# Input norm moved into the state-space input projection, and four staging places in the tail of a hybrid decoder block

## The reference

```python
u = rms_norm(h, norm_g[l])
proj = u @ w_in[l]
q, f_logit, iv, g_hg, u_s, z_s, gate_hg, gate_s5 = jnp.split(proj, _split_points(), axis=-1)
o = hgrn2_mix(...)                      # 8 heads of 128, chunks of 64 steps
y_hg = (rms_norm(o, hg_norm_g) * silu(g_hg)) @ w_o_hg[l]
ys = gelu(s5_mix(u_s, ...))             # 32 groups of 16 channels, 64 complex states each
ys = glu_a * sigmoid(glu_b) * silu(z_s) # glu_a, glu_b from ys @ w_glu + b_glu
y_s5 = ys @ w_o_s5[l]
h = h + (sigmoid(gate_hg) * y_hg + sigmoid(gate_s5) * y_s5) @ w_out[l]
h = h + (p[l] @ w_ple[l]) * sigmoid(rms_norm(h, ple_norm_g[l]) @ w_ple_gate[l])
return rms_norm(h, final_norm_g)
```

## Time and profile before

| | us |
|---|---|
| median of 3 runs | 2375.37 (2375.15 to 2377.81) |
| the profiled execution | 2378.16 |
| its span in the trace | 2376.6 |
| PE busy | 2272.8 (96%) |
| DVE busy | 1199.0 (50%) |
| ACT busy | 919.9 (39%) |

### The profile page before, as it was taken

The page is one execution under the profiler, slowest core; times in us unless marked ns, Lnnn a source line. Parts: engine busy times, 40 slices in busy tenths (PEclk is TensorE's granted clock), DMA queues, the critical chain, the costliest instruction groups (busy, mean ns, idle before and its releaser), DMA issues. The chain is left out here.

```text
span 2376.6 us, 30201 instructions
## 1 busy us (share of the span) xinstructions
PE 2272.8 (96%) x10800; PEld 1836.9 (77%) x10800; DVE 1199.0 (50%) x2230; ACT 919.9 (39%) x1360; POOL 146.8 (6%) x254
## 2 busy tenths in 40 slices
PE   6899999999999997999999999969999999999997
PEld 2688888888888886888777777758887777778775
DVE  5443444343444434111656566546566566665655
ACT  6343444443444434111233333333443354354343
POOL 0000000000000000110111111110001000100100
PEclk8899999999999999999999999989999999999998
DMA  4110101010100100322222222265336435634622
GB/s 160 36 36 23 45 9 44 9 49 18 35 26 26 41 18 14 86 65 85 78 78 87 87 77 80 77 202 167 118 114 212 153 99 177 212 107 135 219 90 79
DMA packets 89267, 206.37 MB, mean 87 GB/s; under 512 B 20832, under 2 KB 30048, under 8 KB 89184
## 3 DMA queue, kind: packets, MB, share of 16 engines
q1 hardware_dynamic: 68432, 139.68, 18.7%
q0 software_dynamic: 20752, 65.57, 8.3%
HBM read 157.87 MB, written 46.14 MB: 86 GB/s over the span
## 5 line engine op out<-in xcount | busy, mean ns | idle before, releaser
L95 PE MATMUL s_ps<-u_hi,s_w_hi 128*128 128x512 f32 x768 | 305.4, 398 | 8.7 <-DVE s_w_lo L875 8.7
L96 PE MATMUL s_ps<-u_lo,s_w_hi 128*128 128x512 f32 x768 | 300.0, 391 | 0.0
L97 PE MATMUL s_ps<-u_hi,s_w_lo 128*128 128x512 f32 x768 | 299.5, 390 | 0.0
L95 PE MATMUL t_ps<-t_oa_hi,t_w_hi 128*128 128x512 f32 x512 | 205.1, 401 | 13.8 <-DVE t_oa_lo L1555 9.9
L96 PE MATMUL t_ps<-t_oa_lo,t_w_hi 128*128 128x512 f32 x512 | 203.0, 396 | 2.5 <-issue 2.5
L97 PE MATMUL t_ps<-t_oa_hi,t_w_lo 128*128 128x512 f32 x512 | 202.7, 396 | 0.0
L1446 DVE TENSOR_TENSOR t_w_lo<-c_raw,t_w_hi 128x1024 fp32r<-128x1024 f32 x136 | 166.5, 1224 | 63.4 <-ACT t_w_hi L1352 63.4
L95 PEld LDWEIGHTS s_ps<-u_hi,s_w_hi 128*128 128x128 f32 x768 | 144.4, 188 | 52.6 <-issue 14.5
L97 PEld LDWEIGHTS s_ps<-u_hi,s_w_lo 128*128 128x128 f32 x768 | 144.5, 188 | 31.1
L96 PEld LDWEIGHTS s_ps<-u_lo,s_w_hi 128*128 128x128 f32 x768 | 144.6, 188 | 28.5
L1352 ACT ACTIVATE t_w_hi<-c_raw 128x1024 fp32r<-128x1024 f32 x136 | 142.4, 1047 | 41.7 <-PE t_ps L97 13.2
(11 more groups left out here) (280 smaller groups left out, 4786.6 us busy)
## 6 DMA issues: line engine op xcount, KB each, us to landing
c_raw<-w_in_in SPq DMA_DIRECT2D x56, 512.0 KB, 3.7
gates_scratch<-s_stage POOLq DMA_DIRECT2D x64, 256.0 KB, 2.7
t_ein<-gates_scratch SPq DMA_DIRECT2D x64, 256.0 KB, 4.4
c_raw<-w_o_hg_in SPq DMA_DIRECT2D x32, 512.0 KB, 5.0
c_raw<-w_out_in SPq DMA_DIRECT2D x32, 512.0 KB, 3.5
c_raw<-w_ple_gate_in SPq DMA_DIRECT2D x32, 512.0 KB, 3.5
c_raw<-w_glu_in SPq DMA_DIRECT2D x16, 512.0 KB, 4.2
t_xa<-o_gated_scratch POOLq DMA_DIRECT2D x32, 256.0 KB, 4.3
```

The source lines that it names most:

```text
L95: pe.matmul(out, w_hi, u_hi, start=first, stop=False)
L96: pe.matmul(out, w_hi, u_lo, start=False, stop=False)
L97: return pe.matmul(out, w_lo, u_hi, start=False, stop=last)
```

## The change

Two parts.

**The head.** `phase_norm_in` is gone; `phase_head` does the norm and the four `u_s` blocks inside the first block of the hgrn phase. x for all 2048 steps lies in `x_xs` (64 KB a partition), is normalised in place, and `u_lo` has the same place in SBUF. For time tile t, TensorE first projects blocks 0 and 1 (into `hg_pf`, `hg_pg`), taking slice k of both as soon as `u_lo` of that slice is there, then blocks 2 and 3 (into `hg_pi`, `hg_pq`). ScalarE drains the four into `n_stage`, and SP stores them. The squares of tile 0 are still summed over all slices by TensorE; those of tiles 1 to 3 are added up by VectorE first (L638, seven additions a tile), so that one matmul with the ones is left a tile, put between slices 2 and 3 of blocks 2 and 3. All four blocks' weights are held at once (two in `c_raw`, two in `n_raw_b`), and the loads of head 0's weights go out in between. The table for Ln and Exp is loaded before the first square. `phase_s5` starts with the `z_s` blocks and has 20 slots.

**The tail.** `t_xa` has four places instead of two, and the waits of its loads follow the split that frees the place.

```diff
-def phase_norm_in(nc, c, a, u_hi, u_lo):
+def phase_head(nc, c, a, xs, u_hi, u_lo):
...
+            for i in range(FIRST):
+                ks = slice(i * KT // FIRST, (i + 1) * KT // FIRST)
+                sp.dma_start(xs[:, ks, 0:TT], a["x"][:, ks, 0:TT]).then_inc(first_in[i], 16)
+            for i in range(2):
+                sp.dma_start(raw[:, i], a["w_in"][UB + i]).then_inc(raw_in[i], 16)
...
+            def normed_blocks(t):
+
+                for half in range(2):
+                    pair = (2 * half, 2 * half + 1)
+                    if t == 0:
+                        pe.wait_ge((w_lo_done, w_lo_b_done)[half], 2)
+                    else:
+                        pe.wait_ge(u_staged, (t - 1) * S5KT + pair[1] + 1)
+                    for k in range(KT):
+                        if half == 0:
+                            pe.wait_ge(lo_done, t * KT + k + 1)
+                        elif k == 3 and t + 1 < NT:
+                            pe.wait_ge(added, (t + 1) * (KT - 1))
+                            pe.matmul((pk, pv)[(t + 1) % 2][:], c["ones"][:].bitcast(F32), sumsq[:, (t + 1) % 2],
+                                      start=True, stop=True).then_inc(xms_done, 1)
+                        for b in pair:
+                            ins = split_matmuls(pe, (pf, pg, pi, pq)[b][:], w_hi[:, b, k], w_lo[:, b, k],
+                                                u_hi[:, k, tile_of(t)], u_lo[:, k, tile_of(t)], k == 0, k == KT - 1)
...
+            for t in range(1, NT):
+                for k in range(KT):
+                    round_u(t, k)
+                    if t + 1 < NT:
+                        square(t + 1, k)
+                    if k == 2:
+                        drain(t - 1, 2)
+                        drain(t - 1, 3)
+                for kind in range(2):
+                    drain(t, kind)
+                    if t == NT - 1:
+                        round_weights(0, kind)
+                if t + 1 < NT:
+                    one_over_rms(t + 1)
...
+            def add_square(t, k):
+                dve.wait_ge(sq_done, t * KT + k + 1)
...
+                before = sq[:, 0] if k == 1 else sumsq[:, t % 2]
+                dve.tensor_tensor(sumsq[:, t % 2], before, sq[:, k % 4], ALU.add).then_inc(added, 1)
...
+            for t in range(NT):
+                dve.wait_ge(xrstd_done, t + 1)
+                for k in range(KT):
+                    normalise(t, k)
+                    if t == 0 and k < 2:
+                        dve.wait_ge(w_hi_done, k + 1)
+                        dve.tensor_tensor(w_lo[:, k], raw[:, k], w_hi[:, k].bitcast(F32), ALU.subtract).then_inc(w_lo_done, 1)
+                    if k >= 1:
+                        split_u(t, k - 1)
+                    if t == 0 and k in (4, 6):
+                        split_late_weights(k // 2 - 2)
+                    elif 1 <= k and 1 <= t < NT - 1:
+                        add_square(t + 1, k)
+                split_u(t, KT - 1)
...
-    NB, U_BLOCKS, Z_BLOCKS = 24, S5KT, 2 * S5KT
+    NB, Z_BLOCKS = 20, S5KT
...
-    BANKS = 6
+    BANKS, XS = 6, 4
...
-        xa = m.sb("xa", [P, 2, TT])
+        xa = m.sb("xa", [P, XS, TT])
...
+                        base = len(XPRO) if isinstance(t, int) and t == 0 else t * len(XBODY) + len(XPRO)
+                        if n >= XS:
+                            splits = base + (n - XS + 1)
+                        elif first:
+                            splits = len(XPRO) - XS + n + 1
+                        else:
+                            splits = base - len(XBODY) + (LAST_USER[n] + 1)
+                        load_xa(splits, n % XS, what, k, t if what == "p" else t + 1)
...
+                    load_xa(n - XS + 1, n % XS, what, k, 0)
```

More of the change, by code:

```diff
@@ L308, in _, with store_u @@
-            prefetched(sp, c, 0, raw_in)
+                if not first:
+                    for kind in range(4):
+                        load_weights(h, kind)
+            def store_u(t, b):
+                sp.wait_ge(u_staged, t * S5KT + b + 1)
+                dst = a["us"].rearrange("(k g) c j n -> k (g c) j n", k=S5KT)[b, :, :, t * NW:(t + 1) * NW]
+                sp.dma_start(dst, stage[:, b].rearrange("p (j n) -> p j n", j=SC)).then_inc(u_stored[b], 16)
+            for i in range(FIRST):
+                ks = slice(i * KT // FIRST, (i + 1) * KT // FIRST)
+                sp.dma_start(xs[:, ks, 0:TT], a["x"][:, ks, 0:TT]).then_inc(first_in[i], 16)
@@ L309, in _ @@
+            for dst, src in ((c["ple_g"][:], a["ple_norm_g"]), (c["fin_g"][:], a["final_norm_g"]), (c["b_glu"][:], a["b_glu"])):
+                sp.dma_start(dst, src).then_inc(late_in, 16)
+            for t in range(NT):
+                for b in range(S5KT):
+                    if t == 1 and b < 2:
+                        load_weights(0, b)
+                    if t == NT - 1 and b >= 2:
+                        load_weights(0, b)
+                    store_u(t, b)
             heads(sp, head)
-            sp.wait_ge(w_lo_done, HEADS * 4)
@@ new lines, in _ @@
+            act.wait_ge(lb_done, 1)
+            one_over_rms(0)
+            for k in range(KT):
+                if k < 2:
+                    act.wait_ge(raw_in[k], 16)
+                    act.activation(w_hi[:, k], raw[:, k], ACT.Copy).then_inc(w_hi_done, 1)
+                round_u(0, k)
+                if 2 <= k < 4:
+                    act.wait_ge(raw_b_in[k - 2], 16)
+                    act.activation(w_hi[:, k], raw_b[:, k - 2], ACT.Copy).then_inc(w_hi_b_done, 1)
+                elif k >= 4:
+                    square(1, k - 4)
@@ new lines, in _ @@
+            for k in range(4, KT):
+                square(1, k)
+            drain(0, 0)
+            drain(0, 1)
+            act.wait_ge(lb_done, 3)
+            act.activation(lb2[:], lb2[:], ACT.Exp).then_inc(lbe_done, 1)
+            one_over_rms(1)
+            for t in range(1, NT):
+                for k in range(KT):
+                    round_u(t, k)
[10 more added lines that the diff above has]
+                    one_over_rms(t + 1)
@@ L482, in _ @@
+            for kind in range(2, 4):
+                drain(NT - 1, kind)
                 round_weights(0, kind)
+            for sem in u_stored:
+                act.wait_ge(sem, NT * 16)
             heads(act, head)
@@ L1161, in loads_after @@
             return t * (UBODY // 2 * 16) + n if body else n
-        def x_buffer(body, what, k, half):
-            return (xn if not body and what == "y" and k >= 2 else xa)[:, half]
         def y_source(k, t):
@@ L1231, in phase_tail, with load_xa @@
         XBODY = [("p", k) for k in range(PLEKT)] + XPRO
+        LAST_USER = [max(n for n in range(len(XBODY)) if n % XS == s) for s in range(XS)]
+        LOADS = [len([n for n in range(len(XBODY)) if n % XS == s]) for s in range(XS)]
         @block.gpsimd
         def _(pool):
-            def load_xa(n, half, what, k, t):
-                pool.wait_ge(x_lo_done, n - 1)
+            def load_xa(splits, slot_, what, k, t):
+                pool.wait_ge(x_lo_done, splits)
                 pool.sem_inc(pool_waits, 1)
@@ L1550, in split_x @@
                 hi, lo = (x[:, k] for x in dict(y=acts_y, o=acts_a, p=acts_p)[what])
-                src, hi = x_buffer(body, what, k, half), hi.bitcast(F32)
+                src, hi = xa[:, half], hi.bitcast(F32)
                 if what == "y":
```

298 lines of the change are left out of this document (139 added, 159 removed).

## The result

The median of the kernel after the change is 2321.48 us (2320.23 to 2324.66, 4 runs), that of before 2376.59 (2375.15 to 2385.66, 4 runs) beside it: ratio 0.9761, 95% interval 0.9738 to 0.9784. The forecast was 2318. Run again beside the last experiments, after took 2325.24 (2321.68 to 2327.14, 5 runs), ratio 0.9767 (0.9749 to 0.9786): the two medians of this one kernel differ by 3.8 us, so a difference of a few us between sets is read from the ratios and the profiles.

What follows compares the result with a forecast made beforehand. TensorE, busy 96% of the span, bounds the kernel; time comes only from idling, low clock or removable work. Head and phase_s5 -33.9, tail -24.5, sum -58.4 us: 2317.0 from the median, forecast 2318 (2310 to 2327).

Steps and rivals of the forecast that it cites:

- the parameter chain: Start of phase_s5: VectorE's parameter work ahead of the z_s products, over 6 us of cover left, costed at nothing.
- Rival 3: Start of phase_s5: parameter chain and first z_s products hold the first slot, 5 to 7 us come back, 2324; chance 0.09.
- the shift of phase_s5: Head's end at 125.0 against head 0's running start at 71.9: later work moves back 53.1 us.
- a cycle of 2.58: Head, tiles 1 and 2: VectorE takes 2.58 us a slice, idle about 0.7 for the square; TensorE needs one every 1.36.
- the clock term: Head, tiles 1 and 2: 3.2 us added for lower clock in TensorE's slow cycle, between nothing and 8.
- rival 4: Head: clock stays at 1.2 GHz from first projection to the head's end, slower than before, 2383; chance 0.04.
- Rival 1: Head: TensorE bounds all of it, slow pairs run at 10.9 us, head 112 instead of 125, 2305; chance 0.16.
- rival 2: Tail: extra places return nothing, as weights and `t_h` fill the DMAs, 2342.5; chance 0.18, whole or larger half.
- The three passages: Tail, from os5 to ohg: four places have inputs ready earlier, returning 7.9 + 4.7 + 7.1 = 19.7 us.
- The prologue: Tail's prologue: `t_h` load goes out some 8 us earlier and the gap of 3.90 goes, returning 6.5 us.
- Given back in ohg: Tail, ohg: o0 and o1 go out behind y3 where weights of out are loaded, costing 1.7 us over three tiles.
- What is left at each passage is about 0.4 us: Tail, each passage from os5 to ohg: with four places the remaining loss is about 0.4 us.

Runs made afterwards that it cites:

- run 3: After, with each addition of a square in tiles 1 and 2 of the head one slice later on VectorE; 2315.10 us, ratio 0.9724 to before.
- run 5: After, with each addition of a square in tiles 1 and 2 of the head issued twice, the second into a spare buffer; 2332.66 us, ratio 0.9802.
- run 1: The new head alone: after, with the last part of before (two staging places); 2346.92 us, ratio 0.9858 to before.
- run 2: The new last part alone: before, with four staging places instead of two; 2359.63 us, ratio 0.9918 to before.

## Why the prediction was right, and where it was not

**Phase_s5** gives back 87.1 us where 87.0 was worked out, and the parameter chain cost nothing: the first z_s blocks run without a wait behind the first. Rival 3 did not happen.

**The head** ends at 123.6, 125.0 was predicted; the shift of phase_s5 is 51.9 for 53.1. That it is nearly right is partly luck: two errors cancel. The mechanism stands: a cycle of 2.58, shown three ways (in the rows, by run 3, which takes the wait out, by run 5, which lengthens it). The terms that were off: VectorE starts tile 1 at 40.96, not 39.7, and without the clock term the sum was 121.8, so the steps are 1.8 short; 1.3 of them are there when VectorE starts tile 1, so they come mostly from tile 0, where the clock is 0.68 in 20 to 30 and the sum left it out. And the clock term of 3.2 for tiles 1 and 2 is nothing: 1.00 in both. The row that it leant on, 0.74 over 17 to 70.3, holds three waits of 3.6 to 4.0 us (the 17.0 of the earlier trace rows less the 5.7 ahead of the window) and the 16.1 ahead of head 0. It says nothing about gaps of 0.9, and run 5 shows that gaps of 1.5 do not bring the slow clock either. For the same reason rival 4 had no ground, and the rule of the Trainium skill that the prediction weighed there (TensorE: Matmul & The Clock Gate, on short idle stretches between groups of matmuls) did not show in these stretches: the trace says 1.00. Rival 1 failed as argued: the addition waits 0.62 us for its square in every slice. Of rival 2 a smaller part came, 6.2 of its 24.5 us.

**The last part** gives -18.3 instead of -24.5, the one term that was mis-sized. The three passages return 8.3 + 5.1 + 7.5 less 0.1 + 5.3 + 0.4 = 15.1, not 19.7: the second still loses 5.3, now to the weights of w_o_hg, for which ScalarE waits 3.75 and 3.07 us ahead of 1954.51 and 1959.69. The prologue returns 3.0, not 6.5: the gap of 3.90 went, two of 2.44 and 1.92 came, on the weights of w_o_s. Given back in ohg: the waits there are 2.42, 2.55 and 0.72 where before has 2.60, 1.90 and 0.67 in the same windows, with low clock 9.3 for 7.0, so 2.3 for the 1.7 predicted. The rest, 2.5 us the other way, lies outside these windows; fewer slow stretches near the end make a part of it (2300:2364 of before has a clock of 0.94, 2248:2312 of after 0.97). In one sentence: the step "What is left at each passage is about 0.4 us" counted the inputs alone and left out the weights, which are what is late next. Against the prediction ScalarE's wait for y2 (4.10) went, down to 0.54 in that tile, behind the new one for w_out, so it gained nothing.

In the profiled executions the sum was -58.4 against -53.5: 6.2 too much in the last part, 1.2 too little in the head. Phase_s5 and the 2.58 us cycle are what the runs confirm; the last part's gain has the right sign and cause at two of three passages, and its error was small enough for the range.

## What to carry to other kernels

An accumulation on VectorE of what ScalarE makes in the same step should take the value of the step before: the reordered addition was worth 6 to 10 us here. More staging places bring loads forward, all of them, so ask which bulk transfer now gets ahead of a small one that is needed first; moving one such transfer behind two small loads was worth 5 to 9 us, and eight places were worse than four by 12. A clock seen behind long gaps is no price for short ones: read it from a row with gaps of the same length.

## What the runs showed of the chip

The lower clock follows single gaps of TensorE, the longer ones more often. Gaps of 0.9 us in each 2.58 and of 1.5 in each 3.18 left the clock at 1.00 throughout. In the last part of the fourteen profiles, leaving out the wait that opens it, the 5 us behind each gap read as follows. Behind 22 gaps of 1.32 to 1.76 us the clock stayed at 1.00, but for one that came 2.6 us after another of 3.21. Of 40 gaps of 1.79 to 2.91 us 21 were followed by a clock of 0.5 to 0.7. Of 45 gaps of 2.97 us and more all were. In the middle group the length does not decide alone: in after, 2.44 us ahead of 1557.29 left the clock at 1.00, and 2.42 ahead of 1811.23 did not (windows of TensorE):

```profile
1557.00:1567.00 10.00, 9.71 (x43) 1.00 0.70 214
1811.00:1821.00 10.00, 9.77 (x36) 0.83 0.58 162
```

What else decides there is not shown. Windows of 10 us show what one fall costs; in before behind the waits at the first and second passage:

```profile
1808.00:1818.00 10.00, 6.36 (x16) 4.69 (x17) 5.35 (x9) 3.36 (x5) 1.08 (x2) 0.66 0.56 181
2008.00:2018.00 10.00, 8.56 (x30) 6.42 (x30) 5.83 (x8) 3.52 (x5) 1.61 (x3) 0.83 0.79 270
```

0.83 is 1.7 us lost, 0.66 is 3.4. Summed over the last part without its last 20 us, where the work runs out (the share not granted, in windows of 10 us), it is 18.7 us in before, 9.5 in after, 20.4 in run 1 and 7.0 in run 2, where the last part took 818, 800, 825 and 795. Half of the 18 us that the last part saved is thus clock behind waits that are gone, and the other half (8.6) the waits themselves, which fell from 34.7 us to 26.1. Of the 6.6 us that run 1 is longer than before, 1.7 is clock.

What stays open: what the moment of t_h against the weights costs when nothing else is changed; why the passage of tile 1 to 2 keeps a wait of about 3 us in every kernel with more than two places, while that of tile 0 to 1 has hardly any; and the share of the prologue's waits that its order of loads could save.
